# Spreading two decay rows between natural transposes, and moving the samples' new scores past a GpSimd product

## The reference, cut to what matters

```python
# prompt
c = jnp.cumsum(logf, axis=1)                          # decay, per token and head
s = einsum('nqhd,nkhd->nhqk', q, k) * scale + c_q - c_k ; mask; softmax; times v
# samples: 2048 cached tokens each, in pages of 128
s_past = einsum('nqhd,nkhd->nhqk', q, k_past) * scale + cnT + suffix
s_new  = einsum('nqhd,nkhd->nhqk', q, k) * scale + cnT - cnT
p = softmax(concatenate([s_past, s_new]))
```

## Time and profile before

| what | us |
|---|---|
| median of 3 runs | 1081.05 |
| the runs | 1074.22 to 1082.45 |
| the profiled execution, its own time | 1082.52 |
| its span | 1080.7 |
| TensorE busy | 885.9 (82%) |
| VectorE busy | 339.7 (31%) |
| GpSimd busy | 257.9 (24%) |
| DMA, mean over the span | 300 GB/s from memory |

### The profile page before, as it was taken

One profiled execution on the slowest core, in us unless ns is written; L12 is line 12 of the kernel. 1 busy time (PEld: TensorE's weight loads), 2 busy tenths in 40 slices (PEclk: granted clock), 3 DMA queues, 4 the chain that ended last, 5 costly groups with the idle time before them and its releaser, 6 DMA issues.

```text
span 1080.7 us, 11539 instructions
## 1 busy us (share of the span) xinstructions
PE 885.9 (82%) x4285; PEld 464.0 (43%) x4285; DVE 339.7 (31%) x627; ACT 193.6 (18%) x391; POOL 257.9 (24%) x341
## 2 busy tenths in 40 slices
PE   5999749997996989579878878787798798894995
PEld 3888426665664445333333323332333333331442
DVE  4899867535234122450000000000000000000652
ACT  3110115423320011211110110110101101110432
POOL 6889655222310000012110111101101101000110
PEclk9999859898987998879898888988988888998898
DMA  9899925167896003606999999999999999997300
GB/s 311 309 355 365 332 94 194 40 255 305 327 418 256 19 39 117 254 13 270 410 408 399 415 403 390 424 402 401 419 409 413 410 398 413 425 394 299 126 40 39
DMA packets 53798, 316.42 MB, mean 293 GB/s; under 512 B 11214, under 2 KB 24078, under 8 KB 33016
## 3 DMA queue, kind: packets, MB, share of 16 engines
q1 hardware_dynamic: 34704, 233.28, 54.1%
q0 software_dynamic: 14480, 76.17, 18.5%
q10 hardware_dynamic: 4576, 6.46, 1.7%
HBM read 309.31 MB, written 14.82 MB: 300 GB/s over the span
## 4 chain that ended last, share of the span: by engine, by line
PE 52%; DMA 32%; DVE 8%; issue 3%; ACT 2%; SPq 1%; POOL 1%; POOLq 0%; DVEq 0%; ACTq 0%
DMA arena<-in_w_up 28%; PE psum L1631 13%; PE psum L1249 8%; PE psum L1501 5%; PE psum L1325 5%; PE psum L1739 5%; DMA arena<-in_w_down 2%; PE psum L1386 2%; PE psum L1646 1%; DVE arena L1897 1%; PE psum L1587 1%; PE psum L1437 1%; PE psum L1365 1%; PE psum L1337 1%; PE psum L469 1%
## 5 line engine op out<-in xcount | busy, mean ns | idle before, releaser
L1631 PE MATMUL psum<-arena 128*64 128x512 f32 x1024 | 273.4, 694 | 80.5 <-DMA arena<-in_w_up 80.5
L1631 PEld LDWEIGHTS psum<-arena 128*64 128x64 f32 x1024 | 92.5, 159 | 237.3 <-issue 236.9
L2289 DVE TENSOR_TENSOR arena<-arena,psum 64x512 f32<-64x512 f32 x32 | 22.1, 692 | 383.4 <-ACT arena L1107 383.4
L1646 PE MATMUL psum<-arena 128*64 128x512 f32 x512 | 116.0, 592 | 2.4 <-DMA arena<-in_w_down 1.9
L1249 PE MATMUL psum<-arena 128*128 128x260 f32 x384 | 86.5, 388 | 0.0
L697 POOL TENSOR_TENSOR arena<-arena 128x2048 f32<-128x2048 f32 x18 | 81.5, 4533 | 1.6 <-ACT arena L870 1.3
L1249 PEld LDWEIGHTS psum<-arena 128*128 128x128 f32 x384 | 73.9, 193 | 12.3 <-issue 0.8
L1325 PE MATMUL psum<-arena 128*128 128x260 f32 x320 | 79.1, 400 | 0.0
L1107 ACT ACTIVATE arena<-psum 64x512 f32<-64x512 f32 x32 | 18.9, 589 | 334.3 <-PE psum L1631 334.3
L762 POOL COPY indices<-row_list 128x1 int32 (+1 forms) x26 | 4.8, 183 | 305.6 <-ACT arena L1113 305.6
L1811 DVE TENSOR_REDUCE arena<-arena 128x32 f32<-128x2048 f32 x32 | 72.0, 2280 | 3.5 <-POOL arena L697 2.4
(11 more groups left out here) (328 smaller groups left out, 884.1 us busy)
## 6 DMA issues: line engine op xcount, KB each, us to landing
arena<-in_w_down SPq DMA_DIRECT2D x32, 2048.0 KB, 25.1
arena<-in_w_gate SPq DMA_DIRECT2D x31, 2048.0 KB, 18.1
arena<-in_w_up SPq DMA_DIRECT2D x31, 2048.0 KB, 22.6
arena<-in_w_in SPq DMA_DIRECT2D x11, 1024.0 KB
arena<-in_x_prompt SPq DMA_DIRECT2D x8, 512.0 KB, 13.7
arena<-in_w_o SPq DMA_DIRECT2D x1, 4096.0 KB
arena<-in_w_ple_gate SPq DMA_DIRECT2D x1, 4096.0 KB, 24.8
arena<-moe_rows SPq DMA_DIRECT2D x4, 1024.0 KB, 7.8
```

What stands on the lines that cost most here:

```text
L1631: last = mm(bank(s)[m * SLOTS:(m + 1) * SLOTS, :], hgT[s][:, k, :], w_gu[s][m][:, k, :], start=(k == 0), stop=(k == DC - 1))
L1646: last = mm(bank(6 + s)[n * SLOTS:(n + 1) * SLOTS, :], actT[s][:, k, :], w_dn[s][:, k, n * BANK:(n + 1) * BANK], start=(k == 0), stop=(k = ...
```

## The change

Three moves. On PE, `spread_ck(0)` goes behind the transposes of k0 and v0, and `spread_ck(1)` behind those of k2 and v2; the wait for the copy of `ct` goes with the first. On ACT, `copy_ck(0)` and `copy_ck(1)` go behind the copy and the store of k0 and of k2. On DVE, `diagonal(0)` goes behind `copy_values(1)`, `diagonal(1)` behind `copy_values(3)`. And DVE's three instructions of the new scores become `new_scores()`, called in step 4 behind `negate_scores(4)`; the signal `smp_req` that PE waits for in step 5 moves with them from the end of `sample_max`. Nothing is added or removed, and the arithmetic is the same.

```diff
@@ ScalarE
+            def copy_ck(h):
+                act.wait_ge(ck_full, h + 1)
...
                 act.dma_start(k_prompt[0, 0, rows].rearrange("t h d -> t (h d)"), k_nat[t % 2]).then_inc(kn_out[t % 2], 16)
+                if t % 2 == 0:
+                    copy_ck(t // 2)
...
-            copy_ck(0)
-            copy_ck(1)
             for s in range(STEPS + 1):
@@ TensorE
+            def spread_ck(h):
+                if h == 0:
+                    pe.wait_ge(free_of("ct"), AT["ct"][1] + 1)
+                released(pe, "ck", h)
+                mm(bank(7), ident[0:HC, h:h + 1].to_broadcast([HC, P]), cT[0:HC, :], start=True, stop=True).then_inc(ck_full, 1)
+
             for t in range(QT):
                 natural(f"k{t}", MT_K, t)
                 natural(f"v{t}", MT_VC, t)
+                if t % 2 == 0:
+                    spread_ck(t // 2)
...
-            spread_ck(0)
-            spread_ck(1)
             for s in range(STEPS + 1):
@@ VectorE
             copy_values(1)
+            diagonal(0)
             multiply_keys(SHARED - 1)
             copy_values(2)
             reduce_keys(SHARED - 2)
             copy_values(3)
+            diagonal(1)
             reduce_keys(SHARED - 1)
             wait_full(dve, "suffix")
             step(v.tensor_tensor(page_suf, fill("suffix")[:, 0:HC], decay[:, PAGE - 1, :], ALU.add))
             dve.nop().then_inc(free_of("suffix"), 1)
-
-            for name in ("ks", "vs"):
-                dve.wait_ge(free_of(name), AT[name][1] + 1)
-            step(v.tensor_tensor(prod_s[0:NB, :], q_s[0:NB, :], k_s[0:NB, :], ALU.mult))
-            step(v.tensor_reduce(new_s[0:NB, :], prod_s[0:NB, :].rearrange("p (h d) -> p h d", h=HC), AX.X, ALU.add))
-            step(v.tensor_tensor(new_s[0:NB, :], new_s[0:NB, :], f_nat[0:NB, QT, :], ALU.subtract))
...
+            def new_scores():
+                for name in ("ks", "vs"):
+                    dve.wait_ge(free_of(name), AT[name][1] + 1)
+                step(v.tensor_tensor(prod_s[0:NB, :], q_s[0:NB, :], k_s[0:NB, :], ALU.mult))
+                step(v.tensor_reduce(new_s[0:NB, :], prod_s[0:NB, :].rearrange("p (h d) -> p h d", h=HC), AX.X, ALU.add))
+                step(v.tensor_tensor(new_s[0:NB, :], new_s[0:NB, :], f_nat[0:NB, QT, :], ALU.subtract))
                 tell(smp_req)
...
-            diagonal(0)
-            diagonal(1)
             for s in range(STEPS):
                 negate_scores(s)
+                if s == 4:
+                    new_scores()
```

More of the change, by code:

```diff
@@ L905, in _ @@
             act.activation(cT[0:HC, :], fill("ct")[0:HC, :], ACT.Copy).then_inc(free_of("ct"), 1)
+            def copy_ck(h):
+                act.wait_ge(ck_full, h + 1)
+                if h >= 4:
+                    act.wait_ge(a_m, 8 * (h // 2 - 1))
+                act.activation(ck_bc[h % 4], bank(7)[:, 0:BLOCK], ACT.Copy, scale=-1.0 / SCALE).then_inc(ck_ready, 1)
             for t in range(QT):
@@ L923, in _ @@
                 act.wait_ge(kn_out[s], 16 * (QT // 2))
[L925 to L929, removed]
             def copy_half(j):
@@ L1296, in _ @@
             done(mm(fill("suffix")[:, 0:HC], later, decay[:, PAGE - 1, :], start=True, stop=True), "suffix")
[L1298 to L1302, removed]
             def spread_gv(t):
@@ L1865, in copy_values, with diagonal @@
                 tell(vn_ready)
+            def diagonal(h):
+                dve.wait_ge(ck_ready, h + 1)
+                if h >= 4:
+                    dve.wait_ge(a_m, 8 * (h // 2 - 1))
+                step(v.scalar_tensor_tensor(out=ck_diag[h % 4].rearrange("p (t n) -> p t n", t=QT),
+                                            in0=bank(7).rearrange("p (t n) -> p t n", t=QT), scalar=-1.0 / SCALE,
+                                            in1=outer(mask, QT), op0=ALU.mult, op1=ALU.add))
+                tell(ck_diag_ready)
             dve.wait_ge(qb_ready, 1)
@@ L1924, in layer_norms @@
                     tell(v_ready)
[L1926 to L1934, removed]
             def negate_scores(s):
```

## The result

| | before | changed |
|---|---|---|
| median | 1081.4 us (1074.22 to 1082.45, 4 runs) | 1063.49 us (1063.07 to 1064.27, 4 runs) |
| profiled execution, its span | 1082.52, 1080.7 | 1064.27, 1062.5 |
| mean granted clock of TensorE | 0.887 | 0.901 |

The ratio is 0.9849, 95% interval 0.9806 to 0.9892: 17.9 us less by the medians, 18.2 us less in the profiled span. The changed kernel was measured twice more beside the kernel before: 0.9816 (0.9794 to 0.9838) and 0.9836 (0.9813 to 0.9858). The change makes the kernel faster, by 1.5 to 1.8%.

The account below looks back on a forecast made before the run. The bound was the serial chain of waits before attention, mostly DVE's stalled subtraction. −18.22 + 1.88 (diagonals) + 1.54 (clock) + 0.30 (new scores) = −14.50 us, so a median of 1066.5, range 1059 to 1075.

Parts of the forecast that it names:

- The mechanism: Before the attention stage, DVE's 8x8 subtraction L1897, with two SBUF inputs, waits for all three POOL products: 12.92 us.
- the clock: PE's sixteen matmuls at the first `rest_step` run at half clock, 7.42 us instead of 5.88: loss 1.54.
- the mark: The attention stage's first `rest_step` on PE, L1325, at 153.50 before the change; expected near 137.1.
- The sign that I had set: In the profile after, the first `rest_step`'s sixteen matmuls should take over 5.9 us.
- Two diagonals: On DVE before the first `rest_step`, each 0.70 us plus a gap of 0.24: 1.88 us added.
- The natural transposes: On PE between 123 and 133, the moved spreads make DVE wait for no transposes; costed at nothing.
- The new scores in step 4: On DVE, 1.65 us just hidden, but two instructions may each wait for a POOL select: 0.3 us lost.
- −18.22: Time leaving the path between DVE's sums at 135.16 and the first `rest_step` at 153.50, one hand-over staying.
- A: Rival: at the stage's start the constant L1905 or first scores stall instead; gain 10.3 less 0.3, 1071.0; chance 5%.
- B: Rival: behind the stage's start, DMA traffic or clock falls eat half the gain, 1073.5; chance 7%.
- C: Rival: spreads keep PE at full clock; sixteen matmuls take 3.71, gain 18.2, 1062.9; chance 8%.
- D: Rival: the new scores stall in step 4 behind POOL's selects, no gain or slower, near 1082; chance 5%.

Follow-up runs that it names:

- operand in PSUM: Kernel before, nothing moved, sum over the heads written to a free PSUM bank so the 8x8 subtraction has one SBUF input; 1067.59 us.
- the gaps: Kernel before, with POOL waiting after the products of chunks 28 and 29 for their own end; 1071.57 us.
- `suffix` read early: Changed kernel with DVE's read of `suffix` ahead of the last diagonal and the sums of chunk 27; 1060.97 us.
- maximum later: Changed kernel with the samples' maximum and `smp_req` moved from step 3 to step 4, behind the reciprocals; 1064.1 us.
- both edits: Changed kernel with `suffix` read ahead of the last diagonal and sums, and the samples' maximum in step 4; 1060.13 us, again 1061.31 us.

## Why the prediction was right, and where its numbers were off

**The mechanism** was the right one. The stall left, the three products stayed back to back, and DVE worked under them. The operand in PSUM shows that two SBUF inputs make the wait (0.15 us instead of 12.92), and the gaps show that the unbroken series makes it long (4.03). The Trainium skill (SBUF — State Buffer, Who interferes with whom) has the first half: a VectorE instruction with two SBUF inputs contends with a GpSimd instruction that reads SBUF. The traces agree. For the length they show more than one instruction of the other engine.

**The step that failed is the clock.** I had charged 1.54 us because the sixteen matmuls at the mark would run wholly at half rate, 7.42 instead of 5.88. They took 5.46. The nearest row, the 5.88 of the earlier trace rows, was itself begun at a granted clock of 0.50 and would have put the term at nothing; 7.42 was worked out from the other rows and was met in no run. The sign that I had set, over 5.9, failed. Windows of PE in the changed kernel (busy, granted clock, DMA share, GB/s):

```profile
128.00:129.00 1.00, 0.00 (x0) 1.00 0.96 381
129.00:130.00 1.00, 0.78 (x4) 0.50 1.13 471
...
138.00:139.00 1.00, 1.00 (x4) 0.50 1.03 356
139.00:140.00 1.00, 1.00 (x6) 0.88 1.10 408
```

The clock was at 0.50 (1.2 GHz) when they began at 135.79, and back at 1.00 (2.4 GHz) within 139 to 140, about halfway through them. In this profile the absence of the 2.80 us of work that stood ahead of them in the earlier trace rows cost nothing. The term was −0.42 instead of +1.54, and this is 1.96 of the 3.7 us by which the profiled span fell more than I had summed. The size of −0.42 is largely chance: with that work ahead the sixteen took 4.98, 5.34, 5.88 and 6.51 us in four kernels, without it 5.31 to 6.81 by the chains of eight profiles. The means are 5.7 and 5.9, little apart beside spreads of 1.5 us, so what the work ahead is worth stays open. Against the 5.88 of the earlier trace rows the eight lie between −0.57 and +0.93: a loss of 1.54 is outside of all of them.

**What came before the mark.** Two diagonals were costed at 1.88 and the mark put at 137.16. It came at 135.79, 1.37 earlier. Of this 1.15 is no effect of the change: the decay rows' matmuls (L1289, ahead of the first moved instruction) start at 117.50, and 1.15 later in the kernel before. Most of the rest is the diagonals. From the start of L1289 to DVE's read of `suffix` are 16.42 us before and 18.11 after, so the two added 1.69: each took 0.70, but the gap behind it is 0.14 and not 0.24. The two other profiles of the changed kernel have the mark at 136.90 and 136.81, within 0.35 of what I had said.

**The natural transposes** made DVE wait nowhere, as said: from v1 on no value tile was late for its copy, up to 133. ACT was a little better off than I had it. I had expected it free about 138, and it had issued its last store by 134.3:

```profile
133.80 0.50 ACTq L928 DMA_DIRECT2D out<-arena  x1
136.38 1.28 ACT L948 ACT_TABLE_LOAD   x1 [6.42 <-DVE arena L1946]
```

It then waited for DVE's maxima, so it was hidden either way.

**The new scores in step 4** were costed at 0.30 with ends of 0 and 1.2. The steps from 144.88 to 172.56 (`L1367`) take 27.68, and those from 163.00 to 190.89 took 27.89 in the kernel before. So they cost the path nothing that can be seen; at ACT the `normalise_p` came 2.10 us behind the first exponential (167.87, 169.97) against 2.00 before.

**The sum.** −18.22 was right, +1.88 should have been +1.69, and the +0.30 of the new scores some 0.1. With these and −0.42 for the clock instead of +1.54, the sum is −16.85 and gives a span of 1063.9; the three profiles have 1062.5, 1064.1 and 1063.0. Of the first one's 1.4 below that, 1.15 lies upstream of the change.

**The rivals.** A, the stall moving to the constant or the first scores, did not come: L1905 took 0.07 and L1946 0.29. The constant even ran 0.97 us before the first product began, so this trace says nothing on how it would fare beside one. The scores of step 1 at 145.25, beside the products, show it for the scores. B, a gain eaten behind the start, did not come either: from the experts' first matmuls to the end are 594.2 us before and 594.6 after, and 592.0 to 594.7 in the profiles of all the experiments. In the stretch between the mark and the experts, though, a lead of 3.5 us can melt, as the profile with only the scores moved shows. C had its time, 1062.9, nearest to the result, but for a wrong reason: PE was not at full clock at the mark. D, a stall in step 4, is refuted by the 0.68 and 0.15 us among the selects.

**The distance.** The forecast of 1066.5 lay 3.0 above the median, and 1061.67 and 1063.7 in the later measurements say that this was no accident of the first. Part of any such distance is chance, since the clock term alone differs by up to 1.5 us between executions. The range, 1059 to 1075, had most of its room on the side that did not come.

## What to carry to other kernels

When a tiny vector instruction is shown for many microseconds, look at GpSimd's timeline beside it and count the instruction's SBUF inputs. If there are two and GpSimd works on SBUF without a pause, either give it one operand in PSUM, or put it behind the series, or give the series a wait. And ask of two edits together what the second is worth once the first is in: here 14.0 and 6.3 made 17.9.

## What was not expected of the hardware

**Who is passed over.** One DVE instruction was held for 12.92 us by three products of some 4.5 us each. With a wait of POOL on its own semaphore after each of the first two, it got in after one (4.03), though the series grew by less than 0.3 us. The one that met a single running product was held 3.62. Selects of 0.2 us, each of which waits for the one before, held nobody. It seems to go the other way too: where the two products of `sample_max` (128x1024, two SBUF inputs, some 1.2 us each) ran beside the 43 selects, in the three profiles with the maximum in step 4, the selects took 16.60 to 16.65 us in place of 14.66. No experiment was made on this.

**The clock comes back at different times.** The same sixteen matmuls, always begun at a granted clock of 0.50 after a pause of PE (in four of the kernels with a spread and scores between), took between 4.98 and 6.81 us. In seven of the profiles, by the chain:

| kernel | start | sixteen matmuls, us | clock back in |
|---|---|---|---|
| changed | 135.79 | 5.46 | 139 to 140 |
| changed, again | 136.90 | 5.64 | 140 to 141 |
| `suffix` read early | 133.83 | 5.37 | 137 to 138 |
| maximum later | 136.45 | 6.81 | 142 to 143 |
| both edits | 132.16 | 6.74 | 138 to 139 |
| changed, third | 136.81 | 5.31 | 139 to 140 |
| both edits, again | 133.62 | 6.67 | 139 to 140 |

By the windows' mean clocks, starting 3.1 us earlier brought the clock back 3.6 us earlier in one kernel (`suffix` read early), and starting 3.2 us earlier brought it back only 0.4 earlier in another (both edits, again). So the first shift paid in full and the second lost 1.4 us of 3.2. It is not the code that differs: up to the mark the kernel with both edits has the same instructions as the one with `suffix` read early (6.74 and 6.67 us against 5.37), and the one with the maximum later the same as the changed kernel (6.81 against 5.31 to 5.64). I have not found what sets it. The Trainium skill (TensorE: Matmul & The Clock Gate, What you observe) says that the moment of the transition varies by half a microsecond either way from run to run. The runs agree that it varies, but by more: for the same instructions up to the mark, the clock was back 3.2 us behind it in one profile (changed, third) and 6.2 in another (maximum later).
